# A fused decoder layer (attention, gated recurrence, expert mixture) on one Trainium2 core: the recurrence's level products inserted two head pairs at a time

## The reference

```python
def step(state, inp):
    qc, kc, vc, gc = inp
    b = jnp.cumsum(gc, axis=2)
    o_inter = jnp.einsum('bhck,bhkv->bhcv', qc * jnp.exp(b), state)
    diff = b[:, :, :, None, :] - b[:, :, None, :, :]
    decay = jnp.exp(jnp.where(causal[:, :, None], diff, -jnp.inf))
    A = jnp.einsum('bhtk,bhtsk,bhsk->bhts', qc, decay, kc)
    o_intra = jnp.einsum('bhts,bhsv->bhtv', A, vc)
    ...
```

## Time and profile before

| | us |
|---|---|
| median of 3 runs | 699.04 |
| the runs | 697.72, 699.04, 700.28 |
| span of the profiled execution | 698.4 |
| TensorE busy in it | 648.2 (93%) |
| VectorE busy | 493.1 (71%) |
| ScalarE busy | 379.0 (54%) |
| GpSimd busy | 94.9 (14%) |
| chain that ended last, TensorE's share | 83% |

### The profile page before, as it was taken

The page is one execution under the profiler, slowest core; times in us unless marked ns, Lnnn a source line. Parts: engine busy times, 40 slices in busy tenths (PEclk is TensorE's granted clock), DMA queues, the critical chain, the costliest instruction groups (busy, mean ns, idle before and its releaser), DMA issues.

```text
span 698.4 us, 10080 instructions
## 1 busy us (share of the span) xinstructions
PE 648.2 (93%) x3906; PEld 526.7 (75%) x3906; DVE 493.1 (71%) x564; ACT 379.0 (54%) x391; POOL 94.9 (14%) x67
## 2 busy tenths in 40 slices
PE   8998999999999999998899999999999999999800
PEld 7787777777677888887888888888888888888600
DVE  4668778875446244249367888888888898898368
ACT  4667225321136664223306877778777777777511
POOL 0032033430000000004043111111111001000112
PEclk9999999999999999999669999999999999999955
DMA  9633111131023003922973999999999999974073
GB/s 335 212 122 122 61 61 61 61 126 61 1 60 122 1 1 142 309 96 86 365 274 143 336 396 387 387 415 381 394 387 392 401 398 403 389 300 173 16 255 120
DMA packets 40736, 152.83 MB, mean 219 GB/s; under 512 B 10900, under 2 KB 11092, under 8 KB 28413
## 3 DMA queue, kind: packets, MB, share of 16 engines
q1 hardware_dynamic: 35708, 139.68, 53.2%
q0 software_dynamic: 4992, 12.66, 4.6%
HBM read 143.84 MB, written 12.68 MB: 224 GB/s over the span
## 4 chain that ended last, share of the span: by engine, by line
PE 83%; DVE 8%; ACT 4%; DMA 2%; issue 2%; POOL 2%; DVEq 0%; SPq 0%; POOLq 0%; ACTq 0%
PE psum L544 22%; PE psum L546 20%; PE psum L545 20%; PE psum L553 3%; PE psum L774 3%; PE psum L655 2%; PE psum L879 2%; PE psum L864 2%; DVE small L1486 1%; PE psum L896 1%; PE psum L752 1%; PE psum L685 1%; PE psum L765 1%; PE psum L838 1%; DVE ring L1668 1%
## 5 line engine op out<-in xcount | busy, mean ns | idle before, releaser
L1460 DVE TENSOR_TENSOR w_lo<-ring,w_hi 128x2048 fp32r<-128x2048 f32 x96 | 218.4, 2290 | 42.5 <-ACT w_hi L1133 42.3
L544 PE MATMUL psum<-w_hi,act_hi 128*128 128x512 f32 x544 | 220.1, 405 | 1.9 <-ACT ring L1054 1.9
L546 PE MATMUL psum<-w_hi,act_lo 128*128 128x512 f32 x544 | 212.6, 391 | 0.0
L545 PE MATMUL psum<-w_lo,act_hi 128*128 128x512 f32 x544 | 212.2, 390 | 0.0
L1133 ACT ACTIVATE w_hi<-ring 128x2048 fp32r<-128x2048 f32 x96 | 182.6, 1918 | 46.8 <-PE psum L546 46.8
L544 PEld LDWEIGHTS psum<-w_hi,act_hi 128*128 128x128 f32 x544 | 102.3, 188 | 27.6 <-issue 3.5
L546 PEld LDWEIGHTS psum<-w_hi,act_lo 128*128 128x128 f32 x544 | 102.1, 188 | 22.2
L545 PEld LDWEIGHTS psum<-w_lo,act_hi 128*128 128x128 f32 x544 | 102.3, 188 | 18.8
L1252 DVE TENSOR_TENSOR w_lo<-ring,w_hi 128x2048 fp32r<-128x2048 f32 x17 | 41.9, 2466 | 35.1 <-ACT w_hi L991 35.0
L991 ACT ACTIVATE w_hi<-ring 128x2048 fp32r<-128x2048 f32 x17 | 32.5, 1913 | 47.8 <-PE psum L546 46.3
L544 PE MATMUL psum<-act_hi,w_hi 128*128 128x512 f32 x128 | 52.0, 406 | 0.4 <-DVE w_lo L1270 0.4
(11 more groups left out here) (204 smaller groups left out, 746.7 us busy)
## 6 DMA issues: line engine op xcount, KB each, us to landing
ring<-in_w_gate SPq DMA_DIRECT2D x32, 1024.0 KB, 7.5
ring<-in_w_up SPq DMA_DIRECT2D x32, 1024.0 KB, 7.6
ring<-in_w_down SPq DMA_DIRECT2D x32, 1024.0 KB, 7.2
ring<-in_w_in SPq DMA_DIRECT2D x13, 1024.0 KB, 5.2
ring<-in_w_o SPq DMA_DIRECT2D x4, 1024.0 KB, 5.0
ring<-pair_dram SPq DMA_DIRECT2D x8, 512.0 KB, 7.5
ring<-in_x SPq DMA_DIRECT2D x2, 1024.0 KB, 6.4
ring<-strip_dram SPq DMA_DIRECT2D x8, 256.0 KB, 4.6
```

What stands on the lines that cost most here:

```text
L544: pe.matmul(dst, lh, rh, start=first, stop=False, skip_group_check=True)
L545: pe.matmul(dst, lh, rl, start=False, stop=False, skip_group_check=True)
L546: return pe.matmul(dst, ll, rh, start=False, stop=last, skip_group_check=True)
L1460: dve.tensor_tensor(w_lo[:, v0 % WBUF, :], ring[:, slot, :], w_hi[:, v0 % WBUF, :].bitcast(F32), ALU.subtract).then_inc(s_lo, 1)
```

## The change

`between` calls `products` behind slots 2 and 10 of units 5 to 10, twice in a row each time: two head pairs in one insertion, 12 insertions in all. Groups go round four banks, 4 to 7 (`4 + g % 4`), in `products` and in `keep`, so group g waits until group g-4 has been copied. Two waits follow from the banks: group 4 also waits for the key transposes to have been copied out of bank 6 and 7, and `key_values(0)`, which takes bank 6 again, waits for the copies of all groups in place of the key copies. The matmuls, the copies and all other engines' instructions are the same and in the same order.

```diff
                 lev, a = g // 4 - 1, g % 4
-                pe.wait_ge(s_copied, g - 1)
+                pe.wait_ge(s_copied, max(g - 3, 4))
+                if g == 4:
+                    pe.wait_ge(s_ketok, T)
                 pe.wait_ge(s_w, lev + 1)
                 pe.wait_ge(s_qz, 8 * lev + 2 * a + 2)
                 for c in range(NCH):
-                    o = psum[64 * (c % 2):64 * (c % 2) + 64, 4 + g % 2, (c // 2) * CH:(c // 2 + 1) * CH]
+                    o = psum[64 * (c % 2):64 * (c % 2) + 64, 4 + g % 4, (c // 2) * CH:(c // 2 + 1) * CH]
...
                 if c == 0:
-                    pe.wait_ge(s_ketok, T)
+                    pe.wait_ge(s_copied, GROUPS)
                     pe.wait_ge(s_evac, 12)
...
-                elif 5 <= u <= 10 and slot % 4 == 1:
-                    products(4 * (u - 4) + slot // 4)
+                elif 5 <= u <= 10 and slot % 8 == 2:
+                    for g in range(2):
+                        products(4 * (u - 4) + slot // 8 * 2 + g)
...
-                    src = bank(4 + g % 2, 256).rearrange("p (i h n t) -> p i h n t", i=T, h=2, t=m)[:, :, par, :, :]
+                    src = bank(4 + g % 4, 256).rearrange("p (i h n t) -> p i h n t", i=T, h=2, t=m)[:, :, par, :, :]
```

## The result

The changed kernel takes 693.86 us in the median of 8 runs (692.66 to 696.57) against 698.38 for the kernel before (8 runs, 697.24 to 700.28): 4.5 us less, ratio 0.9942, 95% interval 0.9924 to 0.9960. A second measurement, on another occasion and with the kernel before beside it, gave 694.39 against 698.92, ratio 0.9946 (0.9924 to 0.9967). The prediction said 695.3, and 693.4 to 698.8.

What follows compares the result with a forecast made beforehand. TensorE, busy 93% of the span, was taken as the bound. Pairing saves 12 x 0.36 = 4.3 us, less 0.6 for waits in the middle, is 3.7: 699.04 - 3.7 = 695.3 us, range 693.4 to 698.8.

Steps and rivals of the forecast that it cites:

- TensorE is the bound, and nothing on it waits in units 5 to 10: Units 5 to 10: TensorE's records cover all 14.24 us of a unit, so its own instructions set the length.
- The passage between large and small matmuls: Level insertions, units 5 to 10: pairing costs 1.30 us against 1.66, saving 0.36 at each of 12 places, 4.3 us.
- Waits in the middle: Second group's three waits, now between small matmuls: met, but costing 0.05 us in each of 12 insertions, 0.6 us.
- Slots: Groups moved to slots 2 and 10 of units 5 to 10: inputs still ready in time, no new wait, cost 0.
- Banks: Four banks: waits for the copy of group g-4, at `key_values(0)` and at group 4 cost 0.
- The saving reaches the end whole: Behind unit 10: everything follows TensorE by semaphores or its own chains, so all 3.7 us should reach the end.
- No gain as a rival: Middle of each pair: second group's first load starts afresh, returning the 0.36 us; 699.0 us, chance 0.15 with the load rule.
- The clock as a small risk on either side: Routing phase: shifted timing may change when TensorE's clock falls; 699.3 us or 693.3 us, chance 0.05 each.
- its bad side: Routing phase, 322 to 324 us: clock falls early, half rate until 328, up to 4 us more, 699.3 us; chance 0.05.

Runs made afterwards that it cites:

- three kernels with one small matmul: Kernel before, each of 24 insertions cut to one matmul (fp32 64 wide, fp32 128 wide, bf16 128 wide), most or all level products left out: 689.28, 691.16, 690.43 us.
- four groups at once: All four groups of a level in one insertion behind slot 8, six insertions in all; 691.08 us, ratio 0.9911 to the kernel before.
- pairs with fillers: Changed kernel plus filler matmuls in two idle stretches of TensorE in the routing phase; 695.14 us, ratio 0.9944 to the kernel before.

## Why the prediction was right

Its range held the time, and the mechanism was the one that it gave; the step of 3.7 us measured 4.5. The median came out 1.4 us below the 695.3: 0.8 by the larger step, and 0.7 because the kernel before itself measured 698.38 in eight runs, not the 699.04 of three. Step by step:

- *TensorE is the bound, and nothing on it waits in units 5 to 10*: right. It is covered 13.49 of 13.49 us in every unit afterwards.
- *The passage between large and small matmuls, 0.36 us at each of 12 places*: right, measured 0.75 / 2 = 0.375 net for each pair. One triple between the groups puts it all back. What the price is made of is known only in part, by the three kernels with one small matmul. The idle time ahead of the weight loads, which the prediction took as its sign, is no measure of it: the bf16 load shows nearly as much (0.26) at a third of the cost.
- *Waits in the middle, 0.05 us an insertion, 0.6 in all*: the wrong term, in size; it is three quarters of the 0.8 us by which the step was too small. Moving them ahead changed nothing. I had read 0.05 from two rows of the attention, by subtracting a modelled record length from one of them; that is too fine a term for such rows. The comparison of equal groups with and without a met wait showed none at the edge, and held in the middle too.
- *Slots*: right. The last queries made in unit 5 end at 91.81 (predicted near 92), and GpSimd's subtraction starts at 85.92 (predicted about 86). The two rows:

```profile
90.95 0.86 DVE L1326 TENSOR_TENSOR misc<-ring 64x256 f32<-64x256 f32 x2
```

```profile
85.92 3.87 POOL L469 TENSOR_TENSOR ring<-ring 128x2048 f32<-128x2048 f32 x1 [17.43 <-PE psum L657]
```

- *Banks*: right, at no cost, and at no gain, as two banks do as well.
- *The saving reaches the end whole*: right, by the equal stretches of 55.05 and 102.6 us.
- *No gain as a rival*, out, by the medians and by the unit's 13.49 us. I had weighed it by the rule that weight loads are pulled ahead of matmuls in flight. The Trainium skill (TensorE: Matmul & The Clock Gate, section "Part 2: What happens when you issue a matmul") says it with two conditions that I left out: the row groups do not conflict, or the load goes to the background weight buffer. The trace agrees for the fp32 block 128 wide (load at 80.03, beside the large matmul), and not for the fp32 block 64 wide (load at 80.47) nor for the bf16 block 128 wide (80.41). The trace doesn't show which condition was met where, so these runs do not tell when a load is pulled ahead, and the bf16 block shows that one that is not can be cheap.
- *The clock as a small risk on either side*: the place was right, the weight too small, and, in the one profile that shows it, the sign of its bad side wrong. The scatter goes with it: the runs of each kernel order nearly by their granted clock, over 3 to 5 us, and one execution's profile differed from the change's own effect by 2.7 us. The early fall that I had priced at 4 us more is what the profile of the changed kernel shows, 3 us behind the first of the two idle times:

```profile
322.00:324.00 2.00, 2.00 (x15) 2.00 (x15) 1.96 (x4) 0.00 (x0) 1.85 (x1) 0.71 0.00 0
```

and its routing stretch was 4.4 us shorter than before, not 4 longer, since the full clock also came back earlier (at 330, against 343 in the kernel before) and the low level held for less time in all: by the mean clocks of the stretch, (1 - 0.79) / 0.5 x 49.07 = 21 us, against (1 - 0.74) / 0.5 x 53.45 = 28. I had counted the early start of the low clock and not its early end. That this execution fell on the shorter side is luck and no merit of the change; the median does not rest on it.

## What to carry to other kernels

In this kernel, small fp32 matmuls with a 64 wide stationary block cost a fixed 0.4 us each time they are put between large ones, and some 0.03 us a record after that. So put as many together as buffers and producers allow, and check the producer's slack (here VectorE's, 0.5 us with four groups at once) before making the groups larger. The key transposes, with blocks of the full width, gained nothing from being paired and can stand alone. When a gain is of the size of the runs' scatter, cut the two traces at the same marks and look where the lengths differ, before believing a difference of spans; a second profile of the same kernel shows how much they differ without any edit.

## What the runs showed of the hardware that I had not expected

- A weight load of a 64 wide fp32 block started 0.32 us behind the start of the large matmul in front, one of a 128 wide fp32 block together with it: 0.476 against 0.262 us for one matmul inserted. A bf16 block 128 wide was loaded late as well, and cost 0.13.
- Three met semaphore waits between matmuls 0.03 us apart cost less than 0.01 us together.
- The granted clock came down while records covered TensorE without a gap (pairs with fillers, 322 to 324 us, 0.67), so a busy row is no sign of a kept clock. It also came down for some 3 us in the changed kernel's first expert triples, behind 28 placement matmuls of 2 columns and 8 transposes: the large matmuls are 0.43 us apart there and not 0.23, which is 1.6 of the 1.7 us by which that stretch was longer. In the second profile of the same kernel the same matmuls stand there and the clock stayed at 1.00, so they alone do not decide it.

```profile
366.44:369.44 3.00, 3.00 (x15) 2.62 (x15) 3.00 (x3) 2.43 (x3) 1.60 (x1) 0.63 0.33 66
```
